# One decoder layer on Trainium2: the prompt values turned by 32x32 block transposes and a trip through memory instead of sixteen TensorE transposes

## What is computed

```
proj = rmsnorm(h) @ w_in                     # 2048 -> q | f | v | g | u, 1024 each
q, k, log_f = silu(q)/sqrt(128), 1 - f, log(f)
for each chunk of tokens:                    # exact causality per token
    o     = (q k^T with decay, causal) @ v  +  (q * decay) @ S
    S_new = decay * S + k^T @ v
h = h + concat(rmsnorm(o) * silu(g), pool(u)) @ w_out
h = h + (silu(gate) * up) @ w_down           # FFN 5632, then a gated embedding and a last norm
```

## Time and profile before

| | |
|---|---|
| median of 3 runs | 1168.29 us (1166.27, 1168.29, 1168.39) |
| the profiled execution | 1166.37 us, of which the span of the trace is 1164.6 |
| TensorE clock granted | 0.997 of full speed |
| PE busy | 1153.4 us (99%) |
| DVE busy | 1001.7 us (86%) |
| ACT busy | 566.9 us (49%) |
| POOL busy | 73.1 us (6%) |
| HBM traffic | 238 MB, mean 204 GB/s |

### The profile page before, as it was taken

The page is one execution under the profiler, slowest core; times in us unless marked ns, Lnnn a source line. Parts: engine busy times, 40 slices in busy tenths (PEclk is TensorE's granted clock), DMA queues, the critical chain, the costliest instruction groups (busy, mean ns, idle before and its releaser), DMA issues.

```text
span 1164.6 us, 30898 instructions
## 1 busy us (share of the span) xinstructions
PE 1153.4 (99%) x12437; PEld 1034.2 (89%) x12437; DVE 1001.7 (86%) x1566; ACT 566.9 (49%) x819; POOL 73.1 (6%) x110
## 2 busy tenths in 40 slices
PE   9999999999999999999999999999999999999997
PEld 7888888888888899899998999989989999999886
DVE  6778799779867898998989989888898999998677
ACT  6545645654555644444444444444444444444544
POOL 2122320101000200000000000000000000000031
PEclk9999999999999999999999999999999999999999
DMA  7767876766566566666666666666666666667595
GB/s 255 240 198 208 237 212 195 233 193 196 182 207 199 181 217 198 196 194 204 216 197 195 193 208 213 194 196 193 213 195 204 215 202 198 204 209 230 175 230 150
DMA packets 199017, 238.07 MB, mean 204 GB/s; under 512 B 12805, under 2 KB 158664, under 8 KB 198672
## 3 DMA queue, kind: packets, MB, share of 16 engines
q1 hardware_dynamic: 192528, 222.13, 61.5%
q0 software_dynamic: 5056, 13.99, 4.2%
q10 hardware_dynamic: 1360, 0.92, 0.3%
HBM read 228.46 MB, written 9.01 MB: 204 GB/s over the span
## 4 chain that ended last, share of the span: by engine, by line
PE 91%; DVE 4%; DMA 2%; issue 1%; ACT 1%; SPq 0%; DVEq 0%; ACTq 0%
PE acc L2343 13%; PE acc L1958 10%; PE acc L1960 10%; PE acc L1962 10%; PE acc L2384 7%; PE acc L2346 6%; PE acc L2345 6%; PE acc L2324 6%; PE acc L2326 6%; PE wrk L2324 4%; PE wrk L2326 4%; PE acc L2387 2%; PE acc L2386 2%; DVE hl L994 2%; PE wrk L2115 1%
## 5 line engine op out<-in xcount | busy, mean ns | idle before, releaser
L994 DVE SCALAR_TENSOR_TENSOR hl<-raw,hl 128x1024 f16<-128x1024 f32 x414 | 493.5, 1219 | 55.4 <-ACT hl L631 52.5
L631 ACT ACTIVATE hl<-raw 128x1024 f16<-128x1024 f32 x414 | 420.7, 1052 | 166.9 <-DMA raw<-in_w_down_dram 91.7
L2343 PE MATMUL acc<-nrm,hl 128*128 128x264 f16 x1344 | 274.8, 276 | 0.0
L1960 PE MATMUL acc<-nrm,hl 128*128 128x264 f16 x920 | 253.9, 276 | 0.0
L1962 PE MATMUL acc<-nrm,hl 128*128 128x264 f16 x920 | 253.9, 276 | 0.0
L1958 PE MATMUL acc<-nrm,hl 128*128 128x264 f16 x920 | 253.9, 276 | 0.0
L2345 PE MATMUL acc<-nrm,hl 128*128 128x264 f16 x672 | 185.5, 276 | 0.0
L2346 PE MATMUL acc<-nrm,hl 128*128 128x264 f16 x672 | 185.5, 276 | 0.0
L2343 PEld LDWEIGHTS acc<-nrm,hl 128*128 128x128 f16 x1344 | 129.0, 98 | 17.8 <-DVE tg L1502 0.2
L2384 PE MATMUL acc<-big,hl 128*128 128x264 f16 x704 | 130.2, 276 | 0.0
L1958 PEld LDWEIGHTS acc<-nrm,hl 128*128 128x128 f16 x920 | 90.2, 98 | 13.3 <-issue 0.3
(11 more groups left out here) (491 smaller groups left out, 2246.7 us busy)
## 6 DMA issues: line engine op xcount, KB each, us to landing
raw<-in_w_gate_up_dram SPq DMA_DIRECT2D x168, 512.0 KB, 4.6
raw<-in_w_down_dram SPq DMA_DIRECT2D x88, 512.0 KB, 4.0
raw<-in_w_in_dram SPq DMA_DIRECT2D x80, 512.0 KB, 4.5
raw<-in_w_out_dram SPq DMA_DIRECT2D x32, 512.0 KB, 5.2
raw<-in_w_ple_gate_dram SPq DMA_DIRECT2D x32, 512.0 KB, 5.3
state<-in_state_hgrn_dram POOLq DMA_DIRECT2D x8, 512.0 KB, 6.9
out_new_hgrn_sample_dram<-state POOLq DMA_DIRECT2D x8, 512.0 KB, 5.2
raw<-in_w_gate_up_dram SPq DMA_DIRECT2D x16, 256.0 KB, 3.7
```

The lines of the kernel that those rows point to most:

```text
L631: nc.scalar.activation(hi[:, st.hl_slot(j, half), :], raw[:, st.raw_slot(j), :], ACT.Copy, scale=WSCALE).then_inc(hi_done, 1)
L994: stt(lo[:, st.hl_slot(j, half), :], raw[:, st.raw_slot(j), :], WSCALE, hi[:, st.hl_slot(j, half), :], ALU.mult, ALU.subtract).then_inc(lo ...
L1960: mm(out, wh, x_lo[:, kt, :], start=False, stop=False)
L2343: mm(out, wh, n_hi[:, kt, :], start=jj == 0 and kk == 0, stop=False, skip_group_check=bool(up))
```

## The change

- The sixteen PE transposes and their four PSUM jobs are gone.
- After its work of block 24 (quad 0) and block 48 (quad 1), DVE turns the quad's values in 32x32 blocks with one instruction of 128x1024 fp32 (`turned_values`) into `vt_blk`, a stretch of `mix` that holds `k_end16` later.
- POOL writes them to memory with four transfers of 128 KB in pieces of 32 floats (`values_out`), waits until all have landed, and reads them back as token rows with four transfers of 128 KB in pieces of 512 bytes (`values_in`), over the old values in `v_all`. For quad 0 the writes stand behind the 16th of the `x_blocks`, the reads behind the 19th; for quad 1 both stand behind the memset of `kv_wide`.
- ACT and DVE make the two halves of `v16` from SBUF, at r = 13 and r = 15 (`V_AT`; blocks 30, 32 and 54, 56) in place of r = 9 and r = 11, once the reads have landed (`vt_in`).

```diff
+V_AT = (13, 15)
...
-        elif _r in (9, 11):
-            JOBS += [(f"vt_{2 * _c + (_r - 9) // 2}", "dve")]
...
+        vt_blk = mix[:, 1536:2560].rearrange("p (k f) -> p k f", f=32)
+        vt_rows = nc.dram_tensor("vt_rows", (QUADS, 4, SEQ, P), F32, kind="Internal").ap()
...
+        def v_rows_of(c, hs):
+
+            return v_all[:, 4 * c + hs.start:4 * c + hs.stop, 0:SEQ].rearrange("p h (a v) -> p h a v", a=2)
...
+            def values_out(c):
+
+                pool.wait_ge(vt_turned, c + 1)
+                for q in range(4):
+                    dst = vt_rows[c].rearrange("h (m i) (q f) -> q i (h m) f", i=32, f=32)[q]
+                    pool.dma_start(dst, vt_blk[32 * q:32 * q + 32]).then_inc(vt_out[c], 16)
+
+            def values_in(c):
+
+                pool.wait_ge(vt_out[c], 16 * 4)
+                for h in range(4):
+                    pool.dma_start(v_all[:, 4 * c + h, 0:SEQ].rearrange("p (a d) -> p a d", a=2),
+                                   vt_rows[c, h].rearrange("(a p) d -> p a d", a=2)).then_inc(vt_in[c], 16)
...
-            x_blocks(range(BUF_BEHIND, X_FIRST))
+            x_blocks(range(BUF_BEHIND, 16))
+            values_out(0)
+            x_blocks(range(16, 19))
+            values_in(0)
+            x_blocks(range(19, X_FIRST))
...
                     nc.gpsimd.memset(kv_wide[1], 0.0).then_inc(zero_ready, 1)
+                    values_out(1)
+                    values_in(1)
...
-                if r in (9, 11):
-                    name = f"vt_{2 * c + (r - 9) // 2}"
-                    wait_job(name)
-                    nc.scalar.activation(v16[:, 0, r - 9:r - 7], wrk[:, JOB[name] % JOB_BANKS, :]
-                                         .rearrange("p (h a v) -> p h a v", h=2, a=2), ACT.Copy, scale=TSCALE).then_inc(tok_hi, 1)
+                if r in V_AT:
+                    act.wait_ge(vt_in[c], 16 * 4)
+                    hs = slice(2 * V_AT.index(r), 2 * V_AT.index(r) + 2)
+                    nc.scalar.activation(v16[:, 0, hs], v_rows_of(c, hs), ACT.Copy, scale=TSCALE).then_inc(tok_hi, 1)
...
+            def turned_values(c):
+
+                if c:
+                    wait_job(f"sf_{c - 1}")
+                nc.vector.transpose(vt_blk, v_all[:, 4 * c:4 * c + 4, 0:SEQ]).then_inc(vt_turned, 1)
...
-                if r in (9, 11):
-                    hs, name = slice(r - 9, r - 7), f"vt_{2 * c + (r - 9) // 2}"
-                    dve.wait_ge(tok_hi, 6 * c + (r - 9) // 2 + 1)
-                    drain(stt(v16[:, 1, hs], bank(name).rearrange("p (h a v) -> p h a v", h=2, a=2), TSCALE, v16[:, 0, hs],
-                              ALU.mult, ALU.subtract), name)
+                if r in V_AT:
+                    hs = slice(2 * V_AT.index(r), 2 * V_AT.index(r) + 2)
+                    dve.wait_ge(tok_hi, 6 * c + V_AT.index(r) + 1)
+                    dve.wait_ge(vt_in[c], 16 * 4)
+                    stt(v16[:, 1, hs], v_rows_of(c, hs), TSCALE, v16[:, 0, hs], ALU.mult, ALU.subtract)
...
                 if b in (24, 48):
                     sample_halves(b // 24 - 1)
+                    turned_values(b // 24 - 1)
...
-            def prompt_v(p):
-
-                out = job(f"vt_{p}")
-                for n in range(4):
-                    last = nc.tensor.transpose(out[:, n * P:(n + 1) * P],
-                                               v_all[:, 2 * p + n // 2, (n % 2) * P:(n % 2 + 1) * P], ident[:])
-                    if n == 3:
-                        last.then_inc(job_done, 1)
-                    yield
```

More of the change, by code:

```diff
@@ L409, in build @@
         sf_out = sem("sf_out")
+        vt_turned = sem("vt_turned")
+        vt_out, vt_in = [sem("vt_out0"), sem("vt_out1")], [sem("vt_in0"), sem("vt_in1")]
         u_turned = sem("u_turned")
@@ L2178, in quad_jobs @@
                     yield from level_scores(c, r // 2 - 1)
-                elif r in (9, 11):
-                    yield from prompt_v(2 * c + (r - 9) // 2)
                 elif r == 16:
```

## The result

The changed kernel takes 1172.11 us (median of 7 runs, 1170.62 to 1176.25), the kernel before 1167.22 (7 runs, 1166.27 to 1168.39). The ratio is 1.0045, 95% interval 1.003 to 1.0061. The change costs 4.5 to 5 us. The prediction had 1169.0 within 1166.0 to 1172.0, and "no difference that can be told" as the likeliest.

A forecast was written before the change was run, and what follows sets the result against it. PE's instruction list was taken as the bound, busy 99% of the span. The sum -1.8 + 0.8 + 0.5 + 2.1 = +1.6 us gave 1168.0 from the profiled execution, 1169.9 from the median; forecast 1169.0, range 1166.0 to 1172.0.

The forecast's parts named there:

- no difference that can be told: Whole kernel: a change within about 0.2% (2.3 us), if any then slower; chance of the same 0.63.
- Part 1: Blocks 26, 28, 50, 52: sixteen transposes leave PE, each worth about 0.11 us, a gain of 1.8 us.
- The rival with 4.4 us: PE: a transpose is worth its duration of about 0.275 us, so the gain is 4.4 us; chance 0.03.
- Part 2: DVE block transposes of 1.22 us: no stop in quad 0, PE stops for 0.8 us in block 51.
- Part 3: Low halves of the values moved: PE stops for 0.5 us in block 56, no cost in quad 0.
- Part 4: Quad 0's trip through memory: values land at 113.5, PE stops for 2.1 us in block 32.
- the term of 2.1 us: Block 32: PE's stop, landing less 111.4, for values landing at 113.5.
- The rival "slower": Quad 0's two trips take longer, landing from 114.3 on, stop from 2.9 us, sum from +2.4; chance 0.32.
- Part 5: Quad 1's trip: reads landed by 196.6 at the latest, ACT needs them at 196.5; fits, without room.
- the middle of both levels: Whole kernel: 1169.0 us, between 1168.0 from the profiled execution and 1169.9 from the median.
- the likeliest case: Block 32: a stop of 0.4 to 2.9 us, total 1166.7 to 1170.6 by both levels; chance 0.43.

The follow-up runs named there:

- e5: Kernel before with each of the sixteen PE transposes issued four times, 48 more in all: 1171.06 us against 1167.25, ratio 1.0029.
- e11: Kernel before with twelve of the sixteen PE transposes left out and nothing in their place: 1167.95 us against 1167.10, ratio 1.0007.
- e4: Changed kernel with V_AT (14, 15) and quad 1's block transpose behind block 49 in place of 48: 1166.22 us against 1167.25, ratio 0.9986.
- e1: Changed kernel with V_AT (14, 15) in place of (13, 15), so values are used later: 1166.82 us against 1166.64, ratio 1.0004.
- e2: Changed kernel with quad 0's writes behind the 15th prompt block and the reads right behind them: 1166.89 us against 1166.64, ratio 1.0001.
- e7: Kernel before, keeping its PE transposes, plus both block transposes and all sixteen transfers, results unused: 1167.62 us against 1167.25, ratio 1.0003.
- e12: The kernel of e4 measured again, against the kernel before: 1166.44 us against 1167.10, ratio 0.9995.
- e10: The changed kernel measured again as it is, against the kernel before: 1171.51 us against 1166.99, ratio 1.0039.
- e9: Changed kernel with quad 0's writes behind the 18th prompt block and the reads right behind them: 1176.83 us against 1166.99, ratio 1.0085.
- e8: The kernel of e4 with DVE's cutting of the prompt's x blocks two blocks earlier: 1166.87 us against 1166.99, ratio 0.9997.
- e3: Changed kernel with quad 0's writes behind the 19th prompt block and the reads right behind them: 1176.72 us against 1166.64, ratio 1.0078.

## Why the prediction was wrong

**Part 1, PE's gain: right.** 0.11 us a transpose (e5, e11), 0.10 over all sixteen (e4): 1.6 to 1.8 us are there. The rival with 4.4 us fell. About half of the gain is lost again by 229.2, where DVE is as late as PE: 0.6 of 1.3 us in e11, 0.8 of 1.6 in e4. For the changed kernel the sum held this loss as its stop in block 56; it did not say that the gain alone brings such a stop.

**Part 2, block transpose: right.** 1.24 us each (1.22 estimated from the earlier trace rows), nothing in quad 0, and in block 51 PE waits for ACT's packing, which comes late behind the level step:

```profile
186.14 0.72 ACT L765 ACTIVATE a<-big 128x256 f32<-128x256 f32 x2 [5.54 <-DVE big L1211]
187.00 0.46 PE L2138 MATMUL wrk<-big,a 128*128 128x128 f32 x2 [0.51 <-ACT a L765]
```

ACT's idle time was 4.41 in the earlier trace rows and is 5.54: the 1.14 us of the transpose, passed on whole. The wait's own row says 0.5, but PE lost more: between 119.8 and 198.8 the changed kernel should gain 0.9 and gains under 0.1, e4 without the stop gains 0.8. So the stop costs 0.7 to 0.8, as the prediction had it, and the row shows only a part of it.

**Part 3, low halves moved: right.** 0.5 us lost between 198.8 and 229.2, all of it at the first matmul of block 56, against 0.5 forecast. In e1, which takes the low half behind the eviction, that stop is gone.

**Part 4, the trip through memory: the step that failed.** Its mechanism was right link by link, and its size was not. Taken apart with the chain above: the writes begin at 99.57 (forecast 99.5) and take 3.13 us to issue (3.1); they have landed at 107.35 (107.9 to 108.5); the last read is issued at 109.76 (109.5 to 110.5). Up to there it is right to about half a microsecond. Then the last read takes 5.39 us to land, where the prediction took some 3.5, between the 2.6 us of the y rows read back and the 4.3 of prompt blocks. The values are there at 115.15, not 113.5, and the term of 2.1 us measured 3.7 (2.8 us of loss by 119.8 and the 0.9 gained ahead of it; e1 against the changed kernel gives the same to 0.1). So the step that failed is the landing time of the last read, too short by 1.9 us.

The 2.6 us was a median over two bursts that have little in common. POOL's reads of y rows, kernel before, the burst from 1116 us and that from 1138.5 us:

```profile
L468 POOL DMA_DIRECT2D big<-y_rows x8: 508/512/518, 1116.0 to 1119.4; - x8
...
DMA to landing us min/median/max: 2.2/5.5/7.7
```

```profile
L468 POOL DMA_DIRECT2D big<-y_rows x8: 508/512/524, 1138.5 to 1141.9; - x8
...
DMA to landing us min/median/max: 2.1/2.3/2.8
```

and the busy shares while they were under way (the last two columns are DMA share and GB/s):

```profile
1116.00:1127.10 11.10, 11.10 (x101) 9.65 (x100) 5.93 (x6) 4.19 (x5) 3.91 (x8) 1.00 0.94 219
1138.00:1144.80 6.80, 6.80 (x80) 6.18 (x78) 6.76 (x12) 3.21 (x5) 3.95 (x8) 1.00 0.45 104
```

The trace of before thus held both prices, and the slow one is that of the fuller queue. The stretch of the trip, before and changed:

```profile
104.00:112.00 8.00, 8.00 (x82) 6.65 (x80) 8.00 (x21) 3.38 (x6) 2.78 (x5) 1.00 0.59 166
```

```profile
104.00:112.00 8.00, 8.00 (x78) 6.85 (x76) 7.71 (x19) 2.44 (x4) 4.96 (x8) 1.00 1.00 288
112.00:116.00 4.00, 3.69 (x33) 3.09 (x31) 0.17 (x1) 0.83 (x3) 1.69 (x3) 1.00 1.01 311
```

The prompt blocks of the earlier trace rows landed at a share of 0.59. The change itself fills it: its own writes and reads come on top of the weights and of the prompt blocks that it pushes back, and the share is 1.00 up to the landing. The price of a transfer was read from the state before the change, and the change altered that state. That the full queue is what makes the last read late fits these rows but is not shown by an experiment: none changed the load alone. The last read of quad 0 took 3.3 us in e2 (share 0.83 meanwhile), 4.0 in e7, 4.2 in e12 and 4.9 to 5.6 in the other seven traces with a trip, so the 5.39 us are near the slow end of what this read takes. The landing times of its four reads:

```profile
DMA to landing us min/median/max: 3.6/4.0/5.4
```

Three of them took 3.6 to 4.1 us, near the 3.5 of the prediction; only the last is slow. It is the maximum that counts, since all four are waited for; the prediction weighed medians. The rival "slower" named exactly this (landing from 114.3 on) and got 0.32; with a landing at 115.15 it gives 1166.37 - 1.8 + 0.8 + 0.5 + 3.75 = 1169.6 for the profiled execution, which was 1170.86.

The Trainium skill (DMA: Bandwidth & Descriptors, Anatomy of one DMA — SWDGE (gpsimd) path) would have these reads land after 2.3 us by its fit, an estimate; here they took 3.6 to 5.4 in a full queue, so the measurement decides against using the fit there. The burst of 64 KB reads at a share of 0.45 above, with 2.1 to 2.8 us, is near it.

**Part 5, quad 1: right, and as tight as it said.** POOL issues the reads at 192.34, they land at 199.20 (196.6 forecast by the times of before, and PE is 2.9 us later here), and nobody waits for them. In the second trace of the same kernel (e10) ACT waits 0.6 us for them without a cost to PE; in e2 and e9 it waits 0.9 and 1.1, and PE's stop in block 56 is 0.7 and 0.8 us in place of 0.3.

**The rest.** From 1155.4 to the end 1.1 us more were lost. There PE waits for DVE, which waits for y rows read back (2.68 us in the changed kernel, 1.76 before). Across the table this stretch differs from before by -0.6 to +1.1 us, and by 0.1 or less in e12, e8 and e7, which make the same transfers: that it belongs to the change is not shown. The median stands 1.3 us above the profiled execution; the prediction had allowed for a level as before had it, 1.9, and then wrote the middle of both levels, 1169.0. From the median, with the measured landing, the same sum is 1171.5. With that one term right, the range around it would have held the time. Why the median lies above the profiled execution stays open. (By its own terms the likeliest case begins at 1166.3, not at the 1166.7 that the prediction states; nothing hangs on it.)

## What to carry to other kernels

When a transpose leaves PE, its price is the distance of starts, 0.11 us here, and a trip through memory in its place took 14 to 17 us for 0.5 MB out and 0.5 MB back. Here that trade came out even at best, and only if nothing asks for the data before the trip has ended at its slowest, which is one number in a schedule. Price a new transfer by the slowest landing in a stretch as loaded as it will be with the transfer in it, and look at each burst by itself before taking a median. And before counting a gain on one engine, look for the next place at which it meets an engine without idle time: here about half of what it had gained was given back there.

## What the runs showed of the hardware

- A stop of PE of 6.7 or 7.8 us (e9, e3) was followed by some 5 and 6 us of work at a granted clock of 0.50, 1.2 in place of 2.4 GHz, which cost another 2.3 and 2.8 us; a stop of 3.5 us left the clock at 1.00 in both traced executions. The Trainium skill (TensorE: Matmul & The Clock Gate, Part 1: The HAM clock gate) has these two levels and lets an idle engine fall to the lower; the trace of e3 agrees.
- Issuing a transfer costs POOL 0.80 us for 128 KB in pieces of 128 bytes, and 0.71 us for 128 KB in pieces of 512 bytes. `values_out` of quad 0 and `values_in` in the changed kernel (duration ns min/median/max):

```profile
L596 POOL DMA_DIRECT2D vt_rows<-mix x4: 797/804/804, 99.6 to 101.9; - x4
...
L602 POOL DMA_DIRECT2D big<-vt_rows x8: 707/713/719, 107.6 to 194.5; - x8
```

- 128x1024 fp32 turned in 32x32 blocks take DVE 1.24 us, on the line through the two smaller sizes of the earlier trace rows.
